# Sorting 88 instead of 80 tokens into the gathered half of a PEER layer's second product

## What is computed

```
def peer_ffn(h, w_q, keys, u, v):           # 288 tokens, D = 2048
    ... idx, gate: 8 heads x top 16 = 128 experts for each token, out of 16384
    ue = u[idx]                              # first product
    act = gelu(einsum('nd,ned->ne', x, ue)) * gate
    ve = v[idx]                              # second product
    return einsum('ne,ned->nd', act, ve)
```

## Time and profile before

| | us |
|---|---|
| median of 3 runs | 2666.61 (2660.39 to 2673.18) |
| the profiled execution, its own time | 2664.87 |
| its span, first to last instruction | 2663.1 |
| first product, from the first gate tile on (1280 to 1918) | 638 |
| second product (1918.2 to 2645.0) | 726.8 |
| what follows it | 18.1 |

### The profile page before, as it was taken

How to read it: one execution, slowest core, us unless ns; L and a number is a source line. 1 busy time by engine, 2 the same in 40 slices (tenths; PEclk the granted TensorE clock), 3 DMA queues, 4 the chain that set the end, 5 groups by cost and what they waited for, 6 DMA issues and landing times.

```text
span 2663.1 us, 56828 instructions
## 1 busy us (share of the span) xinstructions
PE 2542.4 (95%) x23437; PEld 2350.3 (88%) x23437; DVE 1375.4 (52%) x2444; ACT 1082.2 (41%) x1752; POOL 1630.0 (61%) x844
## 2 busy tenths in 40 slices
PE   5899999889979999999999999999989999999997
PEld 3799999657757999999999999999988888888887
DVE  0450355773336455995574010010177777777777
ACT  1333433341223434444333333333444554555555
POOL 0366677012225776888655777777667777777763
PEclk9899999889989999999999999999999999999999
DMA  9987845567855444445555654654588999999884
GB/s 374 395 290 268 274 170 171 183 249 251 261 194 218 170 165 140 158 159 180 180 176 193 239 196 159 257 194 168 192 309 307 323 374 321 332 358 318 311 305 131
DMA packets 213561, 639.92 MB, mean 240 GB/s; under 512 B 16520, under 2 KB 26264, under 8 KB 183832
## 3 DMA queue, kind: packets, MB, share of 16 engines
q1 hardware_dynamic: 176712, 514.54, 55.6%
q0 software_dynamic: 27472, 97.56, 10.1%
q10 hardware_dynamic: 9216, 25.53, 2.4%
HBM read 605.61 MB, written 31.97 MB: 239 GB/s over the span
## 4 chain that ended last, share of the span: by engine, by line
PE 69%; issue 12%; POOL 9%; DVE 5%; DMA 4%; ACT 1%; POOLq 0%; DVEq 0%; ACTq 0%; SPq 0%
PE bank L929 68%; POOL ring_lo L806 8%; DMA kept<-in_peer_v 3%; DVE ring_lo L2791 1%; DVE act_hl L2788 1%; ACT hi_peer L1690 0%; PE bank L932 0%; DVE staged L2853 0%; POOL ring_lo L813 0%; DMA staged<-in_w_ada 0%; DVE staged L2373 0%; DVE staged L2397 0%; ACT act_hl L1690 0%; ACT staged L1687 0%; DVE staged L2781 0%
## 5 line engine op out<-in xcount | busy, mean ns | idle before, releaser
L1690 ACT ACTIVATE hi_peer<-kept 128x1024 fp32r<-128x1024 f32 x544 | 559.2, 1053 | 906.2 <-PE bank L929 775.4
L806 POOL TENSOR_TENSOR ring_lo<-kept,hi_peer 128x1024 fp32r<-128x1024 f32 x288 | 718.1, 2516 | 271.5 <-ACT hi_peer L1690 271.5
L929 PE MATMUL bank<-h_hi,ring_lo 128*128 128x288 f32 x2848 | 839.5, 295 | 0.0
L929 PE MATMUL bank<-act_hl,hi_peer 128*128 128x416 f32 x2048 | 626.1, 371 | 10.5 <-DVE staged L2853 5.6
L929 PE MATMUL bank<-h_hi,hi_peer 128*128 128x288 f32 x2048 | 609.0, 297 | 2.8 <-POOL ring_lo L806 2.5
L929 PE MATMUL bank<-h_lo,hi_peer 128*128 128x288 f32 x2048 | 604.9, 295 | 0.0
L929 PEld LDWEIGHTS bank<-h_hi,ring_lo 128*128 128x128 f32 x2848 | 537.8, 189 | 0.0
L929 PE MATMUL bank<-act_hl,ring_lo 128*128 128x208 f32 x2048 | 529.5, 259 | 0.0
L929 PEld LDWEIGHTS bank<-act_hl,hi_peer 128*128 128x128 f32 x2048 | 385.8, 188 | 50.1 <-issue 37.9
L929 PE MATMUL bank<-staged 64*64 64x64 f32 (+12 forms) x6760 | 388.2, 300 | 37.6 <-issue 19.8
L2788 DVE TENSOR_TENSOR act_hl<-staged,act_hl 128x416 fp32r<-128x416 f32 x256 | 261.8, 1023 | 271.5 <-ACT act_hl L1690 271.0
(11 more groups left out here) (261 smaller groups left out, 3100.6 us busy)
## 6 DMA issues: line engine op xcount, KB each, us to landing
kept<-in_peer_u SPq DMA_DIRECT2D x128, 1024.0 KB, 4.8
kept<-in_peer_v SPq DMA_DIRECT2D x128, 1024.0 KB, 8.7
kept<-in_w_ada SPq DMA_DIRECT2D x64, 1024.0 KB, 8.8
kept<-in_w_in SPq DMA_DIRECT2D x50, 1024.0 KB, 4.9
staged<-in_w_ada SPq DMA_DIRECT2D x32, 1024.0 KB, 6.5
kept<-in_w_adaf SPq DMA_DIRECT2D x32, 1024.0 KB, 5.9
kept<-in_w_out SPq DMA_DIRECT2D x16, 1024.0 KB, 5.1
kept<-in_w_q SPq DMA_DIRECT2D x16, 1024.0 KB, 4.8
```

Source lines behind the costliest of these rows:

```text
L806: pool.tensor_tensor(ring_lo[:, n % RING_SLOTS, cols], ring[n % RING_SLOTS][:, cols], hi_slot(n)[:, cols].bitcast(F32), ALU.subtract).then ...
L929: return pe.matmul(out, lhsT, rhs, start=start, stop=stop)
L1690: return act.activation(out, in_, ACT.Copy)
```

## The change

`GATHERED` goes from 80 to 88, so `VN` from 208 to 200. By the formulas the dense matmuls of the second product get 400 and 200 columns in place of 416 and 208, the gate groups are 50 in place of 52 (`GATE_REST` is [2] in place of [3, 1]), and there are 44 steps in place of 40, between the same tiles 9 and 118. Six sums of 88 columns would not fit a bank of 512, so `TURNED` is 4: the 16 turned blocks lie in banks 0 to 3, and `add_late` has four rounds in place of three.

```
-GATHERED = 80
+GATHERED = 88
 VN = N - GATHERED
...
-        TURNED = 6
+        TURNED = 4
         assert TURNED * GATHERED <= 512
...
                 for kt in range(KT):
-                    mm = matmul(ps[1 + kt // TURNED][:, kt % TURNED * GATHERED:(kt % TURNED + 1) * GATHERED],
+                    mm = matmul(ps[kt // TURNED][:, kt % TURNED * GATHERED:(kt % TURNED + 1) * GATHERED],
                                 late_y[:, kt * P:(kt + 1) * P], order)
...
-                for b in range(3):
-                    kts = slice(TURNED * b, min(TURNED * b + TURNED, KT))
-                    y = ps[1 + b][:, 0:(kts.stop - kts.start) * GATHERED].rearrange("p (k t) -> p k t", t=GATHERED)
+                for b in range(KT // TURNED):
+                    kts = slice(TURNED * b, TURNED * b + TURNED)
+                    y = ps[b][:, 0:(kts.stop - kts.start) * GATHERED].rearrange("p (k t) -> p k t", t=GATHERED)
```

## The result

| | before | changed |
|---|---|---|
| median, us | 2667.07 (20 runs, 2659.04 to 2681.01) | 2676.47 (20 runs, 2668.65 to 2686.31) |
| ratio | | 1.0035, 95% interval 1.0025 to 1.0045 |
| span of the profiled execution | 2663.1 | 2670.8 |

The changed kernel is 9.4 us slower, where 8 us faster was forecast. The measured time lies half a microsecond above the range.

A forecast was written before the change was run, and what follows sets the result against it. TensorE was taken to set the pace, with transfers close behind. Its own work changes by -16.3 us (-22.7 - 1.8 + 7.8 + 0.4), new waits add 8: -8.3 us, so 2658 us, range 2646 to 2676.

The forecast's parts named there:

- What bounds the kernel: Second product: TensorE sets the pace, transfers close behind; 698 us of work in 726.8, some 28 us lost to waits.
- Fewer dense columns: Second product's dense matmuls: 24 columns fewer in each of 2048 pairs, at 0.463 ns a column, save 22.7 us.
- The lower bound: Least saving from fewer dense columns: one column per 1/2.4 ns, 10.0 ns a pair, 20.5 us.
- N/2.4 plus 2.5 ns: Skill's time for back-to-back matmuls: 265 ns a pair, saving 20.5 us; not used, as rows show 300 ns.
- Two gate groups: Tiles with gate groups: two groups fewer take 1.8 us off TensorE.
- four steps: Second product: four more gathered steps at 1.94 us each add 7.8 us on TensorE.
- turning: Turning 88 columns in place of 80 adds 0.4 us to TensorE's work.
- New waits: Second product: more bytes make tile loads about 0.8 us later against their need; +8 us, bounds 0 and +25.
- GpSimd's queue: Gathers and low parts in five tiles and two steps: 25.6 us against TensorE's 27.0, costed at 0.
- the forecast of 38: Steady stretch of the second product: of GpSimd's 79 us wait for ACT, some 38 us are left.
- The rival: GpSimd falls behind, `spread_picks` holds TensorE before even steps: +14 us, 2664 to 2670, chance 0.13.
- Transfers bound: Rival: second product's transfers stay at 333 GB/s, so 174.5 MB take 524 us; 2672 to 2690 us, chance 0.12.

The follow-up runs named there:

- The ladder: Kernel before, another pair of dense matmul widths in each pass of eight tiles; pair 300.6 ns at 416/208, 244.2 at 288/208, 301.2 at 416/144.
- the spacing experiment: Kernel before with its 40 steps 2.53 tiles apart instead of 2.79, same bytes and instructions; ratio 1.0021, +5.6 us.
- the kernel with 96 tokens: 96 gathered tokens, 48 steps, 384/192 columns, activation gathers ahead of the low part of the weights; ratio 1.0111 to the kernel before, 30 us slower.

## Why the prediction was wrong

*What bounds the kernel.* Right: TensorE's pace plus some 28 us of waits make the second product; the reading by starts added up to within half a microsecond in the five traces of the two kernels.

*Fewer dense columns, -22.7 us: the step that failed.* It measured -12.7. The cost of a column was taken as 0.463 ns for all 24, from three widths whose gaps I read one by one, and bounded below by the clock at -20.5. The ladder shows that the narrow matmul's columns cost nothing at all while the wide one keeps its width, and the wide one's 0.44. The lower bound rested on the belief that every streamed column takes its cycle of TensorE's time, but one pair of widths cannot show that. The warning stood in the earlier trace rows: the 416 columns took 32 ns over their cycles at 2.4 GHz (205 against 173) and the 208 only 8, where the earlier trace rows has 13 for 288. I took the sum of the three for a uniform cost instead of asking what the extra 32 ns were.

*The Trainium skill's* N/2.4 plus 2.5 ns ("TensorE: Matmul & The Clock Gate", section "Wait — 56ns, not 53.3ns?") was set aside for its level. Its slope for one wide column, 0.42 ns, is what the ladder shows within 6%; it fails for the narrow ones, where the slope is zero.

*Two gate groups, -1.8; four steps, +7.8; turning, +0.4.* All three came out to 0.1 us: 659.2 to 657.4 us, 1.94 to 1.95 us a step in every trace, and 4.87 in place of 4.56 us from the last matmul of tile 119 to tile 120.

*New waits, +8 us.* The size was near, +10.5 in the traces, and that is luck, for the step behind it did not happen. I had the waits from tile loads that come 0.8 us later against their need. Over all traces the loads hardly changed: landings of 8.8 and 9.2 us before, 9.4, 9.1 and 8.9 after; ACT late for 36 and 39 of them before, for 42, 43 and 36 after. The waits that are not before even steps hardly changed after tile 26 either (4 and 2, then 3, 3 and 2). The growth stands before even steps, from 5 to 17 us. The path of the earlier trace rows, a load that ends in VectorE's split, `spread_picks` and a late step, is among them, but what lengthens it is mostly VectorE's own instructions.

*GpSimd's queue, costed at 0: the second step that failed.* GpSimd stayed off the limit, as counted (its wait for ACT fell to 55 us; the forecast of 38 does not follow from its own slack of 1.4 us a pair of steps, which gives 26), and `lo_front` was nearly always in time (4 us of waits in the stretch). Two things were left out. One is the latency: the fourth activation gather has one tile of 4.7 us between its issue and its use at a distance of five tiles, and lands after 6 us in the median and up to 8.6. It makes 3 to 4 us of the waits before even steps. The other is that VectorE's `spread_picks` and splits do not run beside GpSimd's low part: when they meet, VectorE's instruction lasts until the other has ended. A held `spread_picks` makes some 4 us of them (0.4 and 1.2 before), late splits 8 to 10 (4 to 5 before). Why the denser steps bring more such meetings, the runs do not separate; that they do so without more bytes or steps, the spacing experiment shows. The rival named the wait for `spread_picks` and priced it at +14, which is near what it grew by (12), but gave it only 0.13 and took late loads for its cause.

*Transfers bound.* Did not happen: 343 GB/s with a share of 0.96 and TensorE waiting for something else. The limit of about 358 GB/s for a core that the Trainium skill states ("DMA: Bandwidth & Descriptors", section "Where 436 GB/s comes from") was not reached in the mean; stretches at 394 GB/s occur in the changed kernel too, so the trace does not bear it out as a ceiling.

*The sum.* With 12.7 for 22.7 and 10.5 for 8 the forecast's own arithmetic gives about +4, as the traces do. The columns are 10 of the 12 us between -8 and +4. The medians say 9.4. The remaining 5 us are not explained by the runs.

## What to carry to other kernels

When two matmuls of different widths alternate, read only the time of the pair, and take the price of a column from a run in which that width alone is changed; here a third of the saved columns cost nothing to begin with. Before steps are put closer together, count for each prefetch the distance from its issue to its use in the new tiles and compare it with its latency, not only with the busy time of the queue that issues it. Then look at what the waiting engine did just before: if its own instruction was longer than usual, look for the instruction of another engine that ends with it. A small transfer that something waits for belongs ahead of the long instruction of the same iteration, not behind it: that edit was worth more than the one studied, and also works without it, though here it moved the long instruction as well.

## What was not expected of the hardware

- Alternating 128 x 128 float32 matmuls of W and n columns, each with its own weights, take 118 ns + 0.44 ns x W for the pair, for W from 288 to 416 and n from 144 to 208, whatever n is (within 1 ns in the ladder; the kernel with 96 tokens ran 384/192 at 284.6 ns, 2.4 below it). What the narrow one saves, the wide one's slot takes up again (235 ns for 205 at 416/144).
- VectorE's product of two tiles of 4 columns took 1.37 us in place of 0.17 when GpSimd's subtraction (L813) was running at its start, and ended 19 to 34 ns after it. In the 17 traces but the ladder's there are 57 such cases, and L813 was running at the start of none of the other 303. With the shorter subtraction of `LO_FRONT` = 512 (1.30 us in place of 1.57 in the median) they took 1.09 to 1.26 us.
- Halving the bytes of the row gathers at the same number of descriptors took ACT's wait for tile loads from 112 to 15 us, though GpSimd was as busy as before (392 of 503 us).
- The part of the program ahead of the first spill of activations, the same in all these kernels, ends between 1258 and 1269 us from one trace to the next.
